# A pooling layer's input projection, query norms and pooling put into one block

## What is computed

```
zp = rmsnorm(x) @ w_in_pool                  # 1024 -> 768 pooling channels + 256 memory queries
# per group of 192 channels, trailing windows 2 / 4 / 8 / 16 over [15 earlier rows, this row ...]
s = cs[:, e0:e0 + l, sl] - cs[:, e0 - w:e0 - w + l, sl]
pooled = s / minimum(w, pos + 1) - u
mixed = pooled (per group) @ w_grp * scale
q = rmsnorm per head of 64 (zp[..., -256:]);  att = softmax(q k) v over 256 memory tokens
x = x + concatenate([mixed, att]) @ w_out;   x = x + conv_ffn(rmsnorm(x))
```

## Time and profile before

| | |
|---|---|
| median of 3 runs | 3328.41 us (3324.23 to 3331.62) |
| profiled execution, span from first to last instruction | 3334.1 us |
| TensorE busy in it | 3034.3 us (91%) |
| VectorE, ScalarE, GpSimd busy | 1543.6, 824.3, 946.5 us |
| from the end of the first feed-forward to the last block of layer 1's mixer | 2151.7 to 2416.8 us of the span |

### The profile page before, as it was taken

How to read it: one execution, slowest core, us unless ns; L and a number is a source line. 1 busy time by engine, 2 the same in 40 slices (tenths; PEclk the granted TensorE clock), 3 DMA queues, 4 the chain that set the end, 5 groups by cost and what they waited for, 6 DMA issues and landing times. The chain is left out here.

```text
span 3334.1 us, 51303 instructions
## 1 busy us (share of the span) xinstructions
PE 3034.3 (91%) x19509; PEld 2783.3 (83%) x19509; DVE 1543.6 (46%) x3290; ACT 824.3 (25%) x1524; POOL 946.5 (28%) x412
## 2 busy tenths in 40 slices
PE   5999957888898979899999999992798999999998
PEld 5999944555566669899999999991698999999998
DVE  5311116666654441763562636335426644626353
ACT  4001004666562230431120202111403311202010
POOL 2430000000000014344444444441043444444443
PEclk7997978999997989999999999995899999999999
DMA  4116622000034732111111111110111111111112
GB/s 159 38 31 206 219 78 82 2 1 1 1 109 129 214 101 78 49 43 46 44 38 51 39 49 37 50 38 22 56 45 55 38 38 51 40 49 42 40 46 83
DMA packets 125643, 211.61 MB, mean 63 GB/s; under 512 B 15612, under 2 KB 90346, under 8 KB 124434
## 3 DMA queue, kind: packets, MB, share of 16 engines
q1 hardware_dynamic: 107058, 192.81, 18.2%
q10 hardware_dynamic: 18432, 16.79, 1.6%
HBM read 198.30 MB, written 15.37 MB: 64 GB/s over the span
## 5 line engine op out<-in xcount | busy, mean ns | idle before, releaser
L389 POOL TENSOR_SCALAR weights_high<-weights_whole 128x1024 fp32r<-128x1024 f32 (+2 forms) x176 | 456.9, 2596 | 1205.5 <-PE banks L424 976.2
L420 PE MATMUL banks<-ffn_in_high,weights_high 128*128 128x364 f32 x2112 | 468.5, 330 | 16.7 <-DVE ffn_in_low L300 9.0
L422 PE MATMUL banks<-ffn_in_low,weights_high 128*128 128x364 f32 x2112 | 469.2, 330 | 0.0
L424 PE MATMUL banks<-ffn_in_high,weights_low 128*128 128x364 f32 x2112 | 468.8, 331 | 0.0
L391 POOL TENSOR_TENSOR weights_low<-weights_whole,weights_high 128x1024 fp32r<-128x1024 f32 (+2 forms) x176 | 382.4, 2173 | 26.3 <-issue 11.9
L420 PEld LDWEIGHTS banks<-ffn_in_high,weights_high 128*128 128x128 f32 x2112 | 369.1, 189 | 18.9 <-issue 18.8
L2480 DVE SCALAR_TENSOR_TENSOR conv_out<-conv_ext,conv_w,conv_out 128x1024 f32<-128x1024 f32 x176 | 324.4, 1843 | 111.2 <-ACT conv_out L2416 96.2
L424 PEld LDWEIGHTS banks<-ffn_in_high,weights_low 128*128 128x128 f32 x2112 | 369.4, 189 | 0.0
L422 PEld LDWEIGHTS banks<-ffn_in_low,weights_high 128*128 128x128 f32 x2112 | 369.0, 190 | 0.0
L2416 ACT ACTIVATE conv_out<-conv_ext,conv_b,conv_w 128x1024 f32<-128x1024 f32 (+1 forms) x176 | 138.3, 834 | 545.9 <-DVEq L2471 545.7
L2508 DVE TENSOR_TENSOR x<-x,banks 128x1092 f32 x64 | 82.7, 1292 | 391.8 <-PE banks L424 391.8
(11 more groups left out here) (383 smaller groups left out, 4697.2 us busy)
## 6 DMA issues: line engine op xcount, KB each, us to landing
weights_whole<-in_w_up SPq DMA_DIRECT2D x88, 512.0 KB, 3.5
past_rows<-in_kv_pages SPq DMA_DIRECT2D x160, 128.0 KB, 2.4
z<-in_kv_pages SPq DMA_DIRECT2D x96, 128.0 KB, 2.4
weights_whole<-in_w_down SPq DMA_DIRECT2D x32, 384.0 KB, 3.1
weights_whole<-in_w_down SPq DMA_DIRECT2D x32, 320.0 KB, 2.9
x<-in_cmp_pages ACTq DMA_DIRECT2D x64, 128.0 KB, 5.5
x<-in_cmp_pages SPq DMA_DIRECT2D x64, 128.0 KB, 5.2
cmp_rows<-in_cmp_pages ACTq DMA_DIRECT2D x64, 128.0 KB, 5.6
```

Source lines behind the costliest of these rows:

```text
L389: pool.tensor_scalar(high, whole, 1.0, None, ALU.mult)
L420: pe.matmul(o, wh, high[:, at], start=kk == 0, stop=False)
L422: pe.matmul(o, wh, low[:, at], start=False, stop=False)
L424: last = pe.matmul(o, wl, high[:, at], start=False, stop=kk == len(terms) - 1)
```

## The change

- `project_normed`, `head_norms`, `load_constants` and `pool_mixer` of layer 1 become one block, `pooled_input`. The tiles of w_in1 are multiplied in the order in which pooling needs them, then the two query tiles. DVE writes each product straight into `pool_ext` in three pieces, and forms its window sums before it takes the next one. ACT only places the states and copies the tails.
- The loops over tiles are written out. Group products and the query norms' small products follow the projection on TensorE, interleaved; the norms go in three cuts of 364 columns.
- The buffers of pooling (`ext`, the sums, two pooled tiles, the state) lie in x's own space, once x has been split and squared (`wait_read`) and saved. The last three high and low parts go into the projection's own operands. z is gone; the queries stand in `mix`.
- `conv_ffn(0)` stores x to a scratch tensor in DRAM in eight pieces, behind its last products, without waiting for the landing; `memory_attention` of layer 1 loads it back after its own two loads and waits for it.
- On POOL the splitting of the group weights stands behind `part(2)`; on SP and POOL the waits for the saved and read x stand behind `load(2)` and `part(1)`.

```
+    def wait_read(self, eng):
+
+        eng.wait_ge(self.split, KC)
+        eng.wait_ge(self.squared, KC)
...
-def head_norms(k, z, n, first, layer):
...
+                sp.dma_start(reload[0][:], reload[1]).then_inc(reloaded, 16)
+                sp.wait_ge(reloaded, 16)
 
...
-def pool_mixer(k, z, mix):
+def pooled_input(k, w, w_src, x, x_saved, mix, xn, following):
...
+    order = [0, 1, 4, 2, 3, 5]
+    tiles = order + [NPC, NPC + 1]
+    NTILES = len(tiles)
...
+        ext = [in_spare(W) for _ in range(2)]
+        sa, sb_ = in_spare(W), in_spare(W)
+        held = [in_spare(T) for _ in range(2)]
+        state = in_spare(NPC * B * PST).rearrange("p (c n) -> p c n", c=NPC)
+        rstd = mix[0:HR, 5, :]
...
+        pooled = [held[n % 2] for n in range(NPC - 1)] + [mix[:, 3, :]]
...
+            return (high[:, n, :], low[:, n, :]) if n < 3 else (xn[0][:, n - 3, :], xn[1][:, n - 3, :])
...
+            for name in POOLING:
+                sp.dma_start(c[name][:], k.ins[name]).then_inc(loaded, 16)
+            sp.dma_start(pick[:], k.ins["head_pick"][:, 0:2, 0:HR]).then_inc(loaded, 16)
+            sp.dma_start(spread_w[:], k.ins["head_spread"][0:HR, 0:2, :]).then_inc(loaded, 16)
+            for t in range(w.fetched, NTILES):
+                w.load(sp, t, t % 2, w_src[tiles[t]], cols)
+                if t == w.fetched:
+                    sp.wait_ge(x_saved, 16 * KC)
+                    tokens.wait_read(sp)
+                    sp.dma_start(state, k.ins["pool_state"]).then_inc(state_loaded, 16)
+            w.load_next(sp, NTILES, following)
+            sp.wait_ge(tailed, NPC)
...
+            w.start_pool(pool)
+            pool.memset(mix[:, 3, TE:T], 0.0)
+            for t in range(w.parted, NTILES):
+                w.part(k, pool, t, t // 2, t % 2, cols)
+                if t == w.parted:
+                    pool.wait_ge(x_saved, 16 * KC)
+                    tokens.wait_read(pool)
+                    for n in range(2):
+                        pool.memset(ext[n][:, 0:PST], 0.0)
+                        pool.memset(held[n][:, TE:T], 0.0)
+                    pool.drain().then_inc(zeroed, 1)
+                if t == w.parted + 1:
+                    pool.wait_ge(loaded, 16 * (len(POOLING) + 3))
+                    pool.tensor_scalar(wh[:], raw, 1.0, None, ALU.mult)
+                    pool.drain()
+                    pool.tensor_tensor(wl[:], raw, wh[:].bitcast(F32), ALU.subtract).then_inc(weights_split, 1)
+            w.part_next(k, pool, NTILES, following)
...
+            def tile(t):
+                if t >= 2:
+                    pe.wait_ge(taken, t - 1)
...
+                if n < 2:
+                    pe.wait_ge(taken, NTILES - 1 + n)
+                else:
+                    pe.wait_ge(scaled, n - 1)
+                pe.wait_ge(split, 3 if n < 3 else NPC)
...
+                for m, sq in enumerate((sa, sb_)):
+                    pe.wait_ge(squared, m + 1)
+                    last = pe.matmul(k.ps[0:HR, 6 + x_ % 2, 0:CUT], pick[:, m, :], sq[:, piece(x_)], start=m == 0, stop=m == 1)
+                last.then_inc(summed, 1)
...
+                m, x_ = u % 2, u // 2
+                pe.wait_ge(inverted, x_ + 1)
+                if u >= 2:
+                    pe.wait_ge(normed, u - 1)
...
+            tile(0)
+            tile(1)
+            pe.wait_ge(taken, 1)
+            tokens.pe(pe)
+            for t in range(2, NTILES):
+                tile(t)
+            pe.wait_ge(weights_split, 1)
+            group(0)
+            group(1)
+            head_sum(0)
+            head_sum(1)
+            group(2)
+            pe.wait_ge(rooted, 1)
+            head_sum(2)
+            group(3)
+            pe.wait_ge(rooted, 3)
+            head_spread(0)
+            head_spread(1)
+            group(4)
+            head_spread(2)
+            head_spread(3)
+            head_spread(4)
+            head_spread(5)
+            group(5)
...
+            def take(n):
+                w.wait_product(dve, n)
+                dve.wait_ge(tailed, n - 1)
+                for dst, src, r in pieces(n):
+                    last = dve.tensor_tensor(dst, src, r, ALU.mult)
+                last.then_inc(taken, 1)
+                dve.drain().then_inc(placed, 1)
...
+            dve.wait_ge(zeroed, 1)
+            for n in range(2):
+                w.wait_product(dve, n)
+                for dst, src, _ in pieces(n):
+                    last = dve.tensor_copy(dst, src)
+                last.then_inc(taken, 1)
+            tokens.invert(dve)
+            for n in range(2):
+                for dst, _, r in pieces(n):
+                    dve.tensor_tensor(dst, dst, r, ALU.mult)
+                dve.drain().then_inc(placed, 1)
+            dve.wait_ge(loaded, 16 * (len(POOLING) + 3))
+            for n in range(NPC):
+                if n >= 2:
+                    take(n)
+                sums(n)
+                if 1 <= n <= 3:
                     lower(n - 1)
-            lower(NPC - 1)
+            for m in range(2):
+                w.wait_product(dve, NPC + m)
+                dve.tensor_tensor(in_cuts(mix[:, NPC + m, :]), cut_set(k, m), in_cuts(rms), ALU.mult).then_inc(taken, 1)
+            for n in range(3, NPC):
+                lower(n)
+            for x_ in range(CUTS):
+                dve.wait_ge(rooted, x_ + 1)
+                dve.reciprocal(rstd[:, piece(x_)], rstd[:, piece(x_)]).then_inc(inverted, 1)
+            for u in range(2 * CUTS):
+                m, x_ = u % 2, u // 2
...
+            def round_high(n):
+                act.wait_ge(done, n + 1)
+                act.activation(parts_of(n)[0], pooled[n], ACT.Copy).then_inc(rounded, 1)
...
+                act.activation(sq[:, 0:T], mix[:, NPC + m, :], ACT.Square).then_inc(squared, 1)
...
             for n, ch in enumerate(order):
...
+                act.activation(es[:, :, 0:PST], state[:, ch, :].rearrange("p (b n) -> p b n", b=B), ACT.Copy).then_inc(state_placed, 1)
+                act.wait_ge(placed, n + 1)
+                act.wait_ge(state_placed, n + 1)
+                act.activation(tails[:, ch, 0:PST], ep[:, SEQ:EP], ACT.Copy)
+                act.activation(tails[:, ch, PST:].rearrange("p (b n) -> p b n", b=B), es[:, :, L:ES], ACT.Copy).then_inc(tailed, 1)
+                if 1 <= n <= 3:
+                    round_high(n - 1)
+            act.wait_ge(loaded, 16 * (len(POOLING) + 3))
+            act.wait_ge(done, NPC)
+            square(0, sa)
+            w.wait_product(act, NTILES - 1)
+            for n in range(3, NPC):
                 round_high(n)
-            for n in range(2, NPC):
-                out(n, order[n])
+            square(1, sb_)
+            out(0)
+            out(1)
+            head_root(0)
+            head_root(1)
+            out(2)
+            head_root(2)
+            act.wait_ge(stored, 16)
+            for n in range(3, NPC):
+                out(n)
...
+                    sp.dma_start(result[:, m, :], x[:, m, :]).then_inc(saved or result_stored, 16)
+                if not saved:
+                    sp.wait_ge(result_stored, 16 * KC)
...
         with ExitStack() as l1:
             mix = k.sb(l1, "mixed", [P, NPC + 2, T])
...
-                    xn = two_parts(n, "in1", KC)
-                    project_normed(k, "w_in1", w, ins["w_in1"], NPC + 2, x, xn, k.cst["g_mix"][:, 1, :], (mix[:, 0:2, :], mix[:, 2, :]), z,
-                                   first_two(ins["w_out1"], KC * P))
-                head_norms(k, z[:, NPC:NPC + 2, :], 2, NORMED, 1)
-                pool_mixer(k, z, mix)
-                memory_attention(k, 1, z[:, NPC:NPC + 2, :], mix[:, NPC:NPC + 2, :])
+            with ExitStack() as n:
+                pooled_input(k, w, ins["w_in1"], x, k.x_saved, mix, two_parts(n, "in1", KC), first_two(ins["w_out1"], KC * P))
+            memory_attention(k, 1, mix[:, NPC:NPC + 2, :], mix[:, NPC:NPC + 2, :], reload=(x, k.x_dram))
             parts = two_parts(l1, "mixed1", KC)
             project(k, "w_out1", w, ins["w_out1"], KC, whole_terms(parts, KC),
                     lambda ctx: Split(k, ctx, mix, parts, [(P, i) for i in range(KC)]), add, first_up(1))
```

More of the change, by code:

```diff
@@ L1874, in _, with memory_attention @@
             place(B - 1)
-def memory_attention(k, layer, xq, mix_out, past=None, ahead=0):
+def memory_attention(k, layer, xq, mix_out, past=None, ahead=0, reload=None):
     nc, c = k.nc, k.cst
@@ L2182, in _, with sums @@
-            for n, ch in enumerate(order):
+                dve.tensor_tensor(pl, pooled[n], ph.bitcast(F32), ALU.subtract).then_inc(split, 1)
+            def sums(n):
+                ch = order[n]
                 widths = windows(ch)
-                ep, es = parts(ext[:, n % 2, :])
-                dve.wait_ge(extended, n + 1)
+                ep, es = parts(ext[n % 2])
+                dve.wait_ge(state_placed, n + 1)
                 cp, cs, span, nxt = ep, es, 1, sa
@@ L2255, in _, with head_root @@
+            def head_root(x_):
```

(4 more changed lines are left out.)

224 lines of the change are left out of this document (90 added, 134 removed).

## The result

The changed kernel took **3252.57 us** (median of 4 runs, 3248.86 to 3255.00); on the same chip the kernel before took 3329.66 us (4 runs, 3324.23 to 3331.62). The ratio is 0.9768, with a 95% interval from 0.9753 to 0.9782. The forecast was 3253 us, in a range from 3247 to 3266.

A forecast was written before the change was run, and what follows sets the result against it. It took 114.8 us between projection and pooling's last write, with about 29 us of TensorE work, as the cost. Mixer's end 2371.65 becomes 2296.6: gain 75.0 from span 3334.1, 3259.1, less 5.7: 3253 us, range 3247 to 3266.

The forecast's parts named there:

- part(2) is done at 2185.4: POOL's split for tile 2, after waiting for x to be read, ends at 2185.4; tile 2 starts 2.4 us late.
- Group weights and "part(3)": On POOL the group weights (6.04 + 5.38 us) precede part(3), taken as 6.5 us and done at 2203.6.
- Clock loss 2.1: TensorE loses 2.1 us to a lower clock behind the gap before tile 3, from ends of 1.4 and 2.6.
- +10.2: In the projection, product 7 ends at 2265.7 instead of 2255.5, 10.2 us later.
- Less is lost in front: Rival: part(3) in 5.2, clock loss 1.4, no wait among the spreads; 3 us less, 3250; under 3249 given chance 0.08.
- everywhere, by 0.4 to 2 us: DVE's sums and takes meet each TensorE deadline between products with 0.4 to 2 us to spare, so the sums cost nothing.
- the first rival: DVE becomes the bound: L389 blocks it whole, each part costs 2.1 us more; time 3262; chance 0.22.
- That is 30.5: TensorE's group products, head sums, spreads, waiting and ACT's write behind product 7 take 30.5 us; the block ends at 2296.2.
- Stores "+0.4": Storing x in the feed-forward shows only its last issue, about 0.4 us ahead of the block's end; bounds 0 and 5.2.
- reload "nothing": Loading x back in memory attention costs nothing, ending some 28 us into a stage of 45.0.
- the slower rival: The reload of x holds memory attention; eating the gain needs over 106 us, at 160 us it gives 3382; chance 0.02.
- The last 5.7 us: The runs' median lay 5.7 us below the span; keeping that distance turns the forecast span of 3259.1 into 3253 us.

The follow-up runs named there:

- split_late: The changed kernel with the group weights' rounding on GpSimd moved behind part(4) and their low part behind part(6); 3256.25 us, ratio 0.977.
- act_rounds: The changed kernel with ScalarE instead of GpSimd rounding the group weights, and GpSimd making their low part behind part(3); 3252.04 us, ratio 0.9758.
- dve_more: The changed kernel with one more VectorE operation of 1.28 us for each of the six pooling tiles; 3255.60 us (one run).
- spreads_last: The changed kernel with the last four spreads of the head norms behind the last group product instead of before it; 3249.39 us (one run).
- wait_landing: The changed kernel with the feed-forward block's end waiting until its eight stores of x have landed; 3252.59 us (one run).
- reload_four: The changed kernel loading x back four times in a row instead of once, each load awaited; 3282.06 us (one run).
- split_first: The changed kernel with GpSimd splitting the group weights ahead of its wait for x instead of behind part(2); 3256.06 us (one run).
- before_again: The kernel before the change, unchanged, profiled a second time; 3325.72 us (one run).
- all_three: The changed kernel with the edits of act_rounds and spreads_last, and DVE taking products out of the banks earlier; 3247.87 us, ratio 0.9756.
- norms_last: The changed kernel with all head sums, roots and spreads behind the last of the six group products; 3261.78 us (one run).

## Why the prediction was right, point by point

The sum held to the microsecond: 75.0 us of gain forecast, 75.0 by the rest. Single terms didn't. Of the signs named, product 7 came at 107.9 (some 110), the gap before the fourth tile was 4.8 (5 to 7), none stood before tiles 4 to 7, and the tail took 34.7 (some 30, wrong over 36). Times below are moved to the clock of before (5.39 us later than after's).

- **POOL, "part(2) is done at 2185.4", tile 2 2.4 late.** Measured 2182.5, and tile 2 wasn't late. The last square of ACT ended 2.7 earlier than in the earlier trace rows. The step took it over from before, where `part(2)` stood beside DVE's L308 and held it up; that very part had been moved behind the squares. The trace has it: six L308 in 8.23 us, none held up. The forecast kept a delay whose cause had been moved away.
- **Group weights and "part(3)".** 11.4 us as in the earlier trace rows; `part(3)` 5.9, not 6.5. Tile 3 starts 4.5 us later than before, not 8. split_late and act_rounds show that POOL was its cause, and that without it a take of DVE comes next.
- **Clock loss 2.1.** Tile 3 took 14.6 instead of 12.0: 2.6, the upper end.
- **"+10.2" for product 7.** Measured 107.89 - 100.65 = +7.2. This term of the sum was too large by 3.0, by the first two points. That is the size named in "Less is lost in front", but not by its causes: `part(3)` alone in 5.2 and a clock loss of 1.4 did not come, the earlier end of `part(2)` did.
- **DVE keeps up "everywhere, by 0.4 to 2 us".** Right: no wait before tiles 4 to 7. In the clock of after, the takes end at 2208.1, 2218.7, 2230.8, 2243.4 and 2255.9; the products whose successors need them end at 2209.2, 2221.3, 2233.3, 2245.3 and 2257.3: margins of 1.2 to 2.6 us (the ends used in the expectation of dve_more were some 0.5 too early). The blocking priced at 2.8 per part is borne out. In each of the six parts from `part(3)` on one DVE instruction is held 0.6 to 0.85 us beside L394 and one 1.9 to 2.15 beside L396, 2.7 to 3.0 together (against the same instruction where GpSimd is idle): L2294, 0.28 alone, took 2.43 and ended with its L396. Had L394 blocked for its whole length, as the first rival has it, each part would have cost about 2 more. dve_more bounds the cover at some 2 us. The rival in which DVE becomes the bound was close: 1.3 us per tile would have been enough.
- **"That is 30.5" behind product 7.** Measured 34.4 to the end of ACT's last write (34.7 to the first score). TensorE's order and the side chains were right: up to the end of group 4 it took 22.3 where the terms give 21.4, the last four spreads 3.7 (3.45). The last group took 7.2, not 4.5. It ran for the greater part at the 1.2 GHz level (granted clock 0.50 in the window from 2282 to 2287), which had set in among the eight matmuls of the four spreads ahead of it: the second four took 2.08, and 1.46 in spreads_last at full clock. There, with these spreads behind it, the group ran at the 2.4 GHz level. So this term was too small by 3.9, 2.7 of it in the last group. Full clock had been taken for the whole tail, since TensorE is busy all through it; it was busy, and the clock fell all the same. How much of the group is hit differs: in five versions with the same order it took 6.1 to 6.3.
- **Stores "+0.4", reload "nothing".** 0.45 in TensorE's idle time at the block's start. wait_landing shows the landing's price, 3.2, for the place where it isn't awaited. The reload landed 24.2 us after its issue at 2293.0, in a stage that ended at 2338.7. reload_four rules out the slower rival's mechanism at this size: a load of the same bytes took 13.5 us, where that rival needs over 106.
- **Attention, taken as unchanged,** was 1.5 us shorter: granted clock 1.00 in its first ten us, where it had been 0.83 (both read from windows of ten us). It was not foreseen. The five profiles of changed versions with 1.00 there and one reload (changed, act_rounds, split_late, split_first, wait_landing) all took 46.7; the five others with one reload 47.4 to 50.6. The kernel before isn't fixed either: 48.2 and, in before_again at 0.70, 49.5.
- **The last 5.7 us** for the distance of span to median. As a distance that the kernel keeps they were wrong: after, span and median lie 0.5 apart. The two profiles of before differ by 10.5 us ahead of the first feed-forward and by 0.2 behind it. What the step did was to subtract the gain from the median of the runs, which is a fair base; the span of 3259.1 was missed by 6.0, and so much had gone in the untouched stages.

So -3.0 and +3.9, with -1.5 in attention and +0.6 in all that is left, cancel. The forecast was right by its mechanism, the agreement to half a microsecond is luck. By the timed medians the gain is 77.1 us, with a scatter that is wider than the difference.

On the port: by the Trainium skill (SBUF — State Buffer, Who interferes with whom) a DVE instruction with at most one SBUF input doesn't contend with GpSimd, outside the modes in which DVE uses two ports, and one with two SBUF inputs contends with a GpSimd instruction that reads SBUF. The traces agree on both. The reciprocal (L314, one input) took 6.98 beside L2171 and L2173 as before without them; the copies of the first two products out of the banks (L2302) took 1.41 and 1.42 beside L394 and L396; L300, L2282, L2294 and the first of L2307 (two inputs each) were stretched. The takes (L2260) lie beside no work of GpSimd here and say nothing on it. The lock for the whole instruction that the prediction cites is borne out by L396 and by the long L2171, but not by L394: beside it DVE's instruction lost 0.85 at most, and went on while L394 still ran. Why is open.

## What to carry to other kernels

Work that is moved under products must be counted on its own engine against each deadline (here the take of product t ahead of tile t+2), not against the total: the total fitted, and yet the order of takes and one late split cost 7 us. When a step is moved, look at what it had slowed where it stood, and at what it will slow where it goes: an idle GpSimd isn't free while VectorE reads two operands from SBUF, and ScalarE may be the better place for such work (act_rounds: 1.8 us by it, 7.5 with the new order of takes). Put small float32 products neither ahead of a long full-rate group nor all in one place, and judge them by the granted clock of the stage behind them.

## What the runs showed that wasn't expected

- The granted clock fell to 0.50 with TensorE busy all the time (5.00 of 5.00 us, 2282 to 2287), behind the small matmuls of the spreads in plain float32. Moving them moved it: attention's first ten us had 1.00 (changed), 0.83 (spreads_last), 0.66 (all_three) and 0.50 (norms_last). So a gain in one stage can be paid back in the next, and a version that only shifts the work in time can gain or lose 1.5 us. Why all_three and spreads_last differ, with the same order of products, stays open.
- A DVE operation of 64 columns (0.28 us) took 2.43 beside a GpSimd split, and one of 176 columns (0.34) took 5.73 beside the long rounding in split_late: what was lost went by what was left of GpSimd's instruction, not by DVE's own length.
- Transfers of 4368 KB from DRAM ran beside attention at 322 to 331 GB/s (reload_four) without slowing it: its last gaps lie within 0.1 us of where they lay with one load.
